# Two layers of a hybrid backbone in float32 on one Trainium2 core: the first layer rebuilt, context first, with the latents' attention between the slots of the gather

## The chip, the cores and the metric

The kernel runs on one core of one Trainium2 chip. The metric is the device time of one execution in microseconds; lower is better. Everything is computed in float32.

## The reference

There are 256 context tokens and 256 latent tokens of 1024 elements. Both go through layer 0; layer 1 gives only the latents on. In either layer a token mixer comes first and then the PEER channel mixer, which looks up experts.

```python
# layer 0 mixer: latent attention, 8 heads; context tokens read context only
a = h @ w_in                                   # 1024 -> 384 + 256 + 64
q = rmsnorm(cq) @ w_uq; kv = rmsnorm(ckv) @ w_ukv
s = q_nope @ k_nope.T + rope(q_rope) @ rope(k_rope).T
y = softmax(s * scale) @ v @ w_o; x = x + g_a * y
# layer 1 mixer: grouped-query attention, 8 heads on 2 key heads
# after either mixer: PEER, 8 heads, 16 experts of 16384 for each token and head
t = modulate(rmsnorm(x)); q = t @ w_query
v1, i1 = top_k(q[0] @ sub_k1.T, 16); v2, i2 = top_k(q[1] @ sub_k2.T, 16)
top_s, expert = top_k(v1[:, None] + v2[None, :], 16)
act = gelu(sum(t * u_tab[expert])); x = x + g_f * sum(softmax(top_s) * act * v_tab[expert])
```

The shifts, scales and gates come from silu(c) and silu(c_ctx) times a (1024, 6144) matrix for each layer ("ada"). The latents' attention in layer 0 reads the context's keys and values, but nothing of the context's PEER, so the order of the two is free there.

## The kernel before

The 512 tokens are four chunks of 128: 0 and 1 are context, 2 and 3 latents. The program is a row of phases, with a barrier of all engines behind each.

- `adaln` (L157) loads 8 MB of ada weights (8 tiles of 1 MB, one round) and makes the shift and scale of layer 0's first norm. The row vector goes to DRAM and comes back broadcast over the partitions (`modd`).
- `mla_in` (L300) normalises and transposes all four chunks and projects them with `w_in` (L337).
- `mla_attention` (L552) makes the values (L597) and then, for 8 heads, the queries and keys (L656) and for each of 32 (head, chunk) pairs scores (L457), a maximum (L532), an exponential (L504), transposes (L466) and values (L476). Between the pairs TensorE takes the other 40 ada tiles (L134), three at a time in buffers in `h` and in `arena`.
- `peer(0)` (L694) projects with `w_o` (L847), norms, transposes (L862), makes the first queries and scores (L871, L879) and the first choices of experts, all chunk by chunk, and then runs a loop over 32 units. A unit is one (head, chunk): 16 slots, each a gather by GpSimd (L833) of 128 rows of 8 KB (a row of u and one of v side by side) into one of 16 ring places.
- `gqa_in`, `gqa_attention` and `peer(1)` do layer 1 with 16 units.

Inside a unit the slots go by groups of four (`GRP`). VectorE takes the four dot products of u with the token (L1132); ScalarE the gelu (L979); VectorE multiplies by the gates (L1138); ScalarE writes four 128x128 diagonal matrices (L984), in 8 buffers; TensorE multiplies each with the slot's v rows in two matmuls of 512 columns (L924), which sum 16 slots in one pair of banks; its end frees the places. The choice of the unit after next runs on VectorE in four stages between the groups (L1019 to L1054). `add_output` (L1114, L1117) adds a unit's banks to x. The order of heads is outermost and the chunk inner, so that each unit has its own sum. The loop is a hardware loop of 4 turns of 8 units (`Fori`). In it SyncE loads a tile of the query weights (0.5 MB) and of the keys for half of the units, and TensorE turns each into scores of all four chunks (L886, L894).

```python
                        for g in range(NG):
                            pe.wait_ge(diag_ready, it * (body * NG) + i * NG + g + 1)
                                for n in range(2):
                                    last = nc.tensor.matmul(acc[i % 2][n][:], diag[:, (g % 2) * GRP + k, :], ring[:, kk, D + n * 512:D + (n + 1) * 512],
                                                            start=(kk == 0), stop=(kk == TOPK - 1))
                            last.then_inc(slots_free, 1)
```

## Time and profile before

| what | value |
| --- | --- |
| runs | 2618.32, 2620.34, 2622.73 us; median 2620.34 |
| profiled execution | 2617.42 us, its span 2615.7 us |
| PE busy | 2126.6 us, 81% of the span |
| VectorE busy | 1776.3 us, 68% |
| ScalarE, GpSimd busy | 582.4 us (22%), 848.5 us (32%) |
| DMA moved | 919.71 MB, 352 GB/s in the mean, 805.36 MB of it by the gathers |
| mean granted TensorE clock | 0.924 of 2.4 GHz |

PE is TensorE's matmuls, DVE VectorE, ACT ScalarE, POOL GpSimd and SP SyncE. A float32 matmul of 128 rows stands in the records as two, so 16 records are 8 matmuls. The profile's page cuts the span in 40 slices of 65.4 us; a digit is a tenth of it busy. A wait that the trace calls "issue" is time in which an engine waited for nothing that the profile shows.

### The profile page before, as it was taken

The numbers are of one execution on the slowest core, as the hardware profiler recorded it, in microseconds if no ns is written. First come the engines' busy times: TensorE is split into PE (matmuls) and PEld (weight loads), VectorE is DVE, ScalarE is ACT, GpSimd is POOL, SyncE is SP. The second block draws the span as 40 slices with busy tenths as digits, with TensorE's granted clock in tenths as the row PEclk, the third lists the DMA queues.
The fourth block names the chain that finished last, engine by engine and source line by source line (L and its number), as shares of the span: only waits on it lengthen the run. The fifth ranks groups of instructions, "written<-read, shape, count | busy, mean of one in ns | idle before, by whom it ended". The sixth has DMA issues, their size and how long they took to land. (4 is left out here: it accounts for less than half of the span.)

```text
span 2615.7 us, 21115 instructions
## 1 busy us (share of the span) xinstructions
PE 2126.6 (81%) x5856; PEld 999.3 (38%) x5856; DVE 1776.3 (68%) x4349; ACT 582.4 (22%) x1533; POOL 848.5 (32%) x774
## 2 busy tenths in 40 slices
PE   5899888888778887788877888777859878698786
PEld 2444454333333333333333333334534333344343
DVE  2223357877778877788786887835468777688686
ACT  1222122222212122122212212122212212121212
POOL 0000023443444434444443444200035344254341
PEclk8999999999889998899988999988979989899898
DMA  8467457999999999999999999932179999999996
GB/s 336 157 221 267 173 199 321 421 421 420 422 383 421 421 420 422 376 421 422 420 421 377 421 421 421 404 124 101 41 312 421 420 407 421 410 397 421 387 421 253
DMA packets 136073, 919.71 MB, mean 352 GB/s; under 512 B 15744, under 2 KB 20864, under 8 KB 30128
## 3 DMA queue, kind: packets, MB, share of 16 engines
q0 software_dynamic: 110592, 805.36, 74.5%
q1 hardware_dynamic: 24960, 113.03, 11.5%
q8 instruction: 24, 0.39, 0.1%
q14 instruction: 65, 0.53, 0.1%
q10 hardware_dynamic: 432, 0.40, 0.0%
HBM read 917.58 MB, written 1.15 MB: 351 GB/s over the span
## 5 line engine op out<-in xcount | busy, mean ns | idle before, releaser
L924 PE MATMUL bank<-arena,aux 128*128 128x512 f32 x3072 | 1454.6, 631 | 367.6 <-ACT aux L984 367.5
L833 POOL DMA_INDIRECT arena<-in_uv,small x768 | 848.0, 1104 | 1241.3 <-PE bank L924 941.8
L924 PEld LDWEIGHTS bank<-arena,aux 128*128 128x128 f32 x3072 | 608.8, 202 | 1178.4 <-issue 720.0
L1132 DVE CUSTOM_DVE_ANT_0 arena<-arena,h 128x1024 f32<-128x1024 f32 x768 | 904.6, 1223 | 147.0 <-DMA arena<-in_uv,small 86.3
L979 ACT ACTIVATE small<-small 128x4 f32<-128x4 f32 x192 | 39.4, 205 | 1349.0 <-DVE small L1132 1349.0
L984 ACT ACTIVATE aux<-ident,small 128x128 f32<-128x128 f32 x768 | 245.3, 390 | 59.7 <-DVE small L1138 59.4
L886 PE MATMUL bank<-hT,aux 128*128 128x512 f32 (+1 forms) x512 | 170.3, 486 | 0.0
L822 POOL IOTA small<- 128x16 int32 x2 | 0.3, 134 | 477.5 <-POOLq L53 477.5
L886 PEld LDWEIGHTS bank<-hT,aux 128*128 128x128 f32 x512 | 97.4, 190 | 74.5 <-issue 68.8
L1053 DVE RECIPROCAL small<-small 128x1 f32<-128x1 f32 x52 | 8.5, 164 | 133.6 <-ACT small L992 131.5
L1114 DVE TENSOR_TENSOR bank<-bank,aux 128x512 f32<-128x512 f32 x96 | 67.2, 700 | 47.0 <-PE bank L924 40.5
L847 PE MATMUL bank<-arena,hT 128*128 128x512 f32 x192 | 83.4, 593 | 3.3 <-PEq L53 3.3
L457 PE MATMUL bank<-arena 128*128 128x512 f32 (+1 forms) x160 | 67.5, 539 | 2.1 <-PEq L53 1.4
L1138 DVE TENSOR_TENSOR small<-small 128x4 f32<-128x4 f32 x192 | 31.4, 163 | 54.9 <-ACT small L979 54.9
L1117 DVE TENSOR_TENSOR x<-x,bank 128x512 f32<-128x512 f32 x96 | 65.9, 687 | 3.3
L1132 DVE DVE_READ_ACCUMULATOR2_ANT small<- 128x1 f32 x768 | 63.2, 82 | 0.0
L532 DVE TENSOR_REDUCE small<-bank 128x1 f32<-128x512 f32 (+1 forms) x48 | 28.8, 601 | 50.3 <-PE bank L457 50.3
L979 ACT ACT_TABLE_LOAD x48 | 61.6, 1283 | 1.8 <-PE bank L879 1.0
L992 ACT ACT_TABLE_LOAD x48 | 61.6, 1283 | 0.8
L1233 PE MATMUL bank<-arena,hT 128*128 128x512 f32 x128 | 57.8, 611 | 2.9 <-ACT hT L243 2.9
L656 PE MATMUL bank<-arena 128*128 128x512 f32 x128 | 56.3, 593 | 0.8 <-DVE arena L608 0.8
L1022 DVE MAX8 small<-aux 128x8 f32<-128x128 f32 x156 | 52.9, 339 | 5.4
(143 smaller groups left out, 1420.9 us busy)
## 6 DMA issues: line engine op xcount, KB each, us to landing
h<-in_ada SPq DMA_DIRECT2D x27, 1024.0 KB, 6.0
arena<-in_ada SPq DMA_DIRECT2D x21, 1024.0 KB, 6.9
aux<-in_w_query SPq DMA_DIRECT2D x36, 512.0 KB, 7.9
arena<-in_uv,small POOLq DMA_INDIRECT x768, 21.3
arena<-mod_rows SPq DMA_DIRECT2D x17, 512.0 KB, 6.3
arena<-in_w_o SPq DMA_DIRECT2D x2, 4096.0 KB, 12.1
arena<-in_w_qkv SPq DMA_DIRECT2D x3, 2048.0 KB, 13.0
arena<-in_w_in SPq DMA_DIRECT2D x2, 1536.0 KB, 8.3
```

The costliest lines, as they stand in the source:

```text
L457: last = nc.tensor.matmul(self.bank[S_BANK[u % 2]][:, 0:keys_of(c)], q, k, start=(i == 0), stop=(i == len(terms) - 1))
L833: nc.gpsimd.indirect_dma_start(out=ring[:, k, :], out_offset=None, in_=table, in_offset=bass.IndirectOffsetOnAxis(ap=idx[:, i % 2, k:k + 1 ...
L847: last = nc.tensor.matmul(self.bank[2 * (i % 2) + n][:], self.hT[:, hd, c * P:(c + 1) * P], self.w_o[:, hd, n * 512:(n + 1) * 512], start= ...
L886: last = nc.tensor.matmul(Q_BANK[:, lo:hi], wq[:, k, :], self.hT[:, k, lo:hi], start=(k == 0), stop=(k == KD - 1))
L924: last = nc.tensor.matmul(acc[i % 2][n][:], diag[:, (g % 2) * GRP + k, :], ring[:, kk, D + n * 512:D + (n + 1) * 512], start=(kk == 0), st ...
L979: nc.scalar.activation(w[:, u, ks], a[:, u, ks], ACT.Gelu).then_inc(gelu_done, 1)
L984: last = nc.scalar.mul(diag[:, (g % 2) * GRP + k, :], self.ident[:], w[:, u, g * GRP + k:g * GRP + k + 1])
L992: nc.scalar.activation(gate[:, u, :], top, ACT.Exp, bias=nb, accum_out=es).then_inc(exp_done, 1)
L1114: link(nc.vector.tensor_tensor(s, s, gate_f[:, kind(chunks[c]), n * 512:(n + 1) * 512], ALU.mult))
L1117: link(nc.vector.tensor_tensor(xs, xs, acc[u][n][:], ALU.add))
L1132: last = nc.vector.tensor_tensor_reduce(out=ring[:, k, 0:D], in0=ring[:, k, 0:D], in1=self.h[:, chunks[c] * D:(chunks[c] + 1) * D], scale= ...
L1233: last = nc.tensor.matmul(self.bank[3 * (i % 2) + n][:], self.hT[:, k, c * P:(c + 1) * P], self.w_qkv[:, n, k, :], start=(k == 0), stop=(k ...
```

## The change

Phases 1 to 4 (`adaln`, `mla_in`, `mla_attention`, `peer(0)`) become one phase, `trunk`, without a barrier in it and without a hardware loop. Layer 1 stays as it is, line for line.

- **Context first.** Only chunks 0 and 1 are normed, projected and attended ahead of the first unit (8 heads, each for both context chunks at once). All 48 ada tiles are taken in this part, 8 first, 10 in the projections and 3 in each of 10 steps of the attention; they use 7 places and from tile 35 on 3. `x` is loaded between ada tiles 3 and 4.
- **Queues.** The stores of the modulation rows and the broadcast loads of the context part go from SyncE to GpSimd. `w_o` is loaded twice (whole behind ada tile 34, then for the latents in four parts of 1 MB), each head's `w_uq` and `w_uk` twice (0.5 MB a head), and each query tile of layer 0 twice (16 MB where 8 MB were).
- **Units.** Of the 32 units the 16 of the context come first, and the chunk is outermost: units 0 to 7 are chunk 0, 8 to 15 chunk 1, then 2 and 3. The 8 units of a chunk sum into one pair of banks, and the chunks alternate between two pairs (banks 0, 1 and banks 2, 3), so `add_output` runs 4 times and no more 32 times.
- **Combine.** The diagonals stay 128x128. There are 4 buffers, written one by one; TensorE waits for two, does 4 matmuls and frees two ring places.
- **Ring.** GpSimd waits before each gather. Gathers use 7 places in units 0 to 2, 10 up to unit 15 and 15 from unit 16 on.
- **Latents between slots.** `Turns` gives out the latents' work at positions: position 2k is in the k-th group (behind the first pair on TensorE, behind the second dot product on VectorE), position 2k + 1 at its end. Norm transposes at 1 and 3, projections at 5 to 16, values at 18 and 20, head 0 from 22, heads 3 to 7 one in 6 positions from 50 on, `w_o` at 83 to 90, the second norm at 91 to 104. A unit is 8 positions. So the latents' part fills units 0 to 12.
- **Queries.** `job_of` gives queries of one head for two chunks: heads 2 to 7 of the context in units 0 to 4, the latents' heads in units 13 to 20, each 32 matmuls of 256 columns. The tops of a head's second chunk are kept in `vals`.

```diff
+    def run(self, position):
+        while self.due is not None and self.due <= position:
+            self.due = next(self.program, None)
...
+        for n in range(SLOTS):
+            pos = n % 7 if n < 48 else n % 10 if n < SLOTS // 2 else n % 15
+            self.turn.append(1 + self.place.count(pos))
+            self.place.append(pos)
+            self.freed_by.append(holder.get(pos))
+            holder[pos] = n
...
-            self.adaln()
-            self.layer(0)
-            self.layer(1)
+            self.trunk()
+            self.gqa_in()
+            self.gqa_attention()
+            self.peer(1, list(range(CC, NC)))
...
@@ trunk, SyncE @@
+                for n in range(15, steps):
+                    ada(n)
+                    if n == 34:
+                        sp.wait_ge(ada_used, 32)
+                        sp.dma_start(self.w_o_first, d["w_o0"]).then_inc(w_o_loaded, 16)
+                    if n >= 24 and n % 3 == 0 and (n - 24) // 3 + 4 < H:
+                        sp.wait_ge(kp_done, (n - 24) // 3 + 1)
+                        head((n - 24) // 3 + 4, False)
...
+                def part(i):
+                    sp.dma_start(self.w_o_part[i], d["w_o0"][:, :, 256 * i:256 * i + 256]).then_inc(part_loaded[i], 16)
...
+                sp.wait_ge(kp_done, H + 6)
+                part(0)
+                sp.wait_ge(evac_done, 1)
+                part(2)
+                sp.wait_ge(kp_done, 2 * H)
+                part(1)
@@ trunk, GpSimd @@
+                    pool.wait_ge(rows_done, r + 1)
+                    self.ada_store(layer, i, rows[r % 2], pool, stored)
...
+                    pool.wait_ge(stored, 16 * NQ * (r + 1))
+                    if r == 0:
+                        for j, seg in enumerate((SC_A, SH_A)):
+                            pool.dma_start(self.mix_rows[:, j], self.mod_row(0, CON, seg)).then_inc(mix_ctx_loaded, 16)
...
+                for n in range(SLOTS):
+                    unit, k = divmod(n, TOPK)
...
+                    pos, prior = self.place[n], self.freed_by[n]
+                    if prior is not None:
+                        pool.wait_ge(slots_free, prior // 2 + 1)
...
+                    nc.gpsimd.indirect_dma_start(
+                        out=ring[:, pos, :], out_offset=None, in_=table,
+                        in_offset=bass.IndirectOffsetOnAxis(ap=self.idx[:, unit % 4, k:k + 1], axis=0)).then_inc(gathered[pos], 16)
@@ trunk, TensorE @@
+                ctx_proj(0)
+                for u in range(H + 2):
+                    if u < H:
+                        ctx_scores(u)
+                    if u + 1 < H:
+                        ctx_proj(u + 1)
+                    if 1 <= u <= H:
+                        ctx_transposes(u - 1)
+                    if u >= 2:
+                        ctx_values(u - 2)
+                    for n in range(18 + 3 * u, 21 + 3 * u):
+                        ada(n)
...
+                    for hd in range(3, H):
+                        b = 50 + 6 * (hd - 3)
+                        yield b
+                        scores_of(hd)
+                        yield b + 1
+                        values_of(hd - 1)
+                        if hd + 1 < H:
+                            yield b + 2
+                            q_of(hd + 1)
+                            yield b + 3
+                            k_of(hd + 1)
+                        yield b + 4
+                        transposes_of(hd)
...
+                            pe.wait_ge(diag_ready, s + 2)
...
+                                    last = nc.tensor.matmul(bank[2 * (n // H % 2) + m][:], self.dg[:, (s + o) % 4, :], ring[:, at, D + 512 * m:D + 512 * m + 512],
+                                                            start=first and o == 0, stop=last_one and o == 1)
+                            last.then_inc(slots_free, 1)
+                            if half == 0:
+                                fill.run(2 * (n * NG + g))
...
+                        elif j is not None:
+                            if g < 2:
+                                query_job(j, g)
+                            if g == 2:
+                                score_job(j)
+                        fill.run(2 * (n * NG + g) + 1)
@@ trunk, ScalarE @@
+                    def exps(hd):
+                        act.wait_ge(mx_done, H + hd + 1)
+                        if hd:
+                            act.wait_ge(pt_done, H + 2 * hd)
...
+                        for k in range(g * GRP, (g + 1) * GRP):
+                            s = n * TOPK + k
+                            if s >= 4:
+                                act.wait_ge(slots_free, (s - 4) // 2 + 1)
+                            nc.scalar.mul(self.dg[:, s % 4, :], ident[:], self.w[:, n % 2, k:k + 1]).then_inc(diag_ready, 1)
...
+                        fill.run(2 * (n * NG + g))
@@ trunk, VectorE @@
+                    def maxima(hd):
+                        dve.wait_ge(s_done, H + hd + 1)
...
+                    for hd in range(3, H):
+                        b = 50 + 6 * (hd - 3)
+                        yield b + 1
+                        maxima(hd)
+                        yield b + 3
+                        normalise(H + hd, probs_lat, TOK)
+                        if hd + 1 < H:
...
+                                op0=ALU.mult, op1=ALU.add, accum_out=self.a[:, u, k:k + 1])
+                            if k % GRP == 1:
+                                fill.run(2 * (n * NG + g))
...
+                        ks = slice(g * GRP, (g + 1) * GRP)
+                        dve.wait_ge(gelu_done, n * NG + g + 1)
+                        nc.vector.tensor_tensor(self.w[:, u, ks], self.w[:, u, ks], self.gate[:, n % 4, ks], ALU.mult).then_inc(w_ready, 1)
+                        if g == 0 and n % H == 0 and n:
+                            dve.wait_ge(slots_free, n * H)
+                            add_output(c - 1)
```

What moved shows in the order of the instructions. First TensorE in the attention of layer 0, before; L656 projects queries and keys of a head for 512 tokens, L457 are scores, L466 transposes of probabilities, L476 values, L134 an ada tile:

```order
49 L457 MATMUL bank<-arena 128x256 x2
50 L466 MATMUL bank<-ident,aux 128x128 x4
51 L476 MATMUL bank<-aux,arena 128x128 x4
52 L134 MATMUL bank<-arena,aux 32x512 x4
53 L134 MATMUL bank<-h,aux 32x512 x4
54 L457 MATMUL bank<-arena 128x256 x2
55 L656 MATMUL bank<-arena 128x512 x8
56 L466 MATMUL bank<-ident,aux 128x128 x2
57 L476 MATMUL bank<-aux,arena 128x128 x4
58 L134 MATMUL bank<-h,aux 32x512 x4
59 L457 MATMUL bank<-arena 128x512 x2
```

TensorE for a latent head in units 6 to 9, now; L852 is the combine (4 rows a pair of slots), L746 and L747 scores, L763 values, L516 and L524 queries and keys, L754 transposes:

```order
197 L852 MATMUL bank<-arena,aux 128x512 x8
198 L746 MATMUL bank<-aux 128x512
199 L747 MATMUL bank<-arena,aux 128x512
200 L746 MATMUL bank<-aux 128x512
201 L747 MATMUL bank<-arena,aux 128x512
202 L852 MATMUL bank<-arena,aux 128x512 x4
203 L763 MATMUL bank<-h,arena 128x256 x4
204 L852 MATMUL bank<-arena,aux 128x512 x4
205 L516 MATMUL bank<-arena 128x256 x6
206 L852 MATMUL bank<-arena,aux 128x512 x4
207 L524 MATMUL bank<-arena 128x512 x2
208 L852 MATMUL bank<-arena,aux 128x512 x4
```

The attention's matmuls stood together, with ada tiles between them; now each piece of a latent head stands between two pairs of slots of the combine.

VectorE at the end of a group of dot products, before (L1138 gates, L1046 and L1048 the last stage of a choice, L1053 and L1054 gates of the next, L1058 scores out of the bank, L1132 the next dot product):

```order
367 L1137 REGISTER_ALU
368 L1138 TENSOR_TENSOR small<-small 128x4
369 L1046 SCALAR_TENSOR_TENSOR small<-small 128x16
370 L1048 TENSOR_SCALAR small<-small 128x1
371 L1142 REGISTER_ALU
372 L1053 RECIPROCAL small<-small 128x1
373 L1054 TENSOR_SCALAR small<-small 128x16
374 L1057 ISA
375 L1058 COPY aux<-bank 128x4x128
376 L1131 ISA
377 L1132 ISA arena,small<-arena,h 128x1024
```

The same place in unit 7, now (L1455 gates, L1332 and L1335 the choice, L1390 and L1391 the maxima of a latent head's scores, L1447 the next dot product):

```order
775 L1455 TENSOR_TENSOR small<-small 128x4
776 L1332 SCALAR_TENSOR_TENSOR small<-small 128x16
777 L1335 TENSOR_SCALAR small<-small 128x1
778 L1390 TENSOR_REDUCE small<-bank 128x1 x2
779 L1391 TENSOR_SCALAR small<-small 128x2
780 L1447 ISA arena,small<-arena,h 128x1024
```

Between two groups of dot products VectorE now has the maxima, which wait for TensorE's scores of that head.

## Rows read from the trace of the kernel before

**Rows 1.** The page, part 2: 40 slices of the span
```profile
GB/s 336 157 221 267 173 199 321 421 421 420 422 383 421 421 420 422 376 421 422 420 421 377 421 421 421 404 124 101 41 312 421 420 407 421 410 397 421 387 421 253
```

**Rows 2.** Windows: length, busy (instructions) of PE, PEld, DVE, ACT, POOL, PEclk, DMA, GB/s
```profile
119.00:302.00 183.00, 174.05 (x864) 88.27 (x864) 57.02 (x153) 44.12 (x113) 0.00 (x0) 1.00 0.64 236
430.00:1712.00 1282.00, 1058.97 (x2368) 457.88 (x2367) 1002.07 (x2436) 285.11 (x762) 541.45 (x490) 0.93 1.00 413
```

**Rows 3.** Timeline of SP, POOL, DVE: start, length, engine, line, operation
```profile
27.85 1.18 SPq L129 DMA_DIRECT2D mod_rows<-aux  x4
31.88 0.81 SPq L225 DMA_DIRECT2D arena<-mod_rows  x2
330.83 0.29 DVE L1019 MAX8 small<-aux 128x8 f32<-128x128 f32 x1
340.86 0.17 DVE L1046 SCALAR_TENSOR_TENSOR small<-small 128x16 int32<-128x16 f32 x1
342.22 1.08 POOL L833 DMA_INDIRECT arena<-in_uv,small  x1 [39.70 <-issue]
343.61 0.95 POOL L833 DMA_INDIRECT arena<-in_uv,small  x1 [0.31 <-issue]
```

**Rows 4.** Timeline of PE ahead of and in the attention
```profile
25.21 1.07 PE L134 MATMUL bank<-arena,aux 128*32 128x512 f32 x8 [1.42 <-DMA arena<-in_ada]
44.93 12.33 PE L337 MATMUL bank<-arena,hT 128*128 128x384 f32 x32 [0.77 <-ACT hT L243]
71.71 10.59 PE L337 MATMUL bank<-arena,hT 128*128 128x384 f32 x32 [0.72 <-ACT hT L243]
241.28 7.03 PE L656 MATMUL bank<-arena 128*128 128x512 f32 x16
250.35 1.99 PE L457 MATMUL bank<-arena 128*128 128x512 f32 x4
```

**Rows 5.** Timeline of PE from `w_o` to the first queries
```profile
302.48 20.84 PE L847 MATMUL bank<-arena,hT 128*128 128x512 f32 x48 [1.89 <-PEq L53]
323.44 1.09 PE L862 MATMUL bank<-ident,h 128*128 128x128 f32 x8
325.35 3.81 PE L871 MATMUL bank<-hT,aux 128*128 128x128 f32 x32 [0.82 <-ACT hT L957]
```

**Rows 6.** The gathers of L833 from 340 to 425 us, issue to landing
```profile
DMA to landing us min/median/max: 5.6/8.9/15.4
```

**Rows 7.** Timeline of DVE, ACT and PE in the loop of layer 0
```profile
400.13 1.22 DVE L1132 CUSTOM_DVE_ANT_0 arena<-arena,h 128x1024 f32<-128x1024 f32 x1
401.91 1.28 ACT L984 ACTIVATE aux<-ident,small 128x128 f32<-128x128 f32 x4 [0.32 <-DVE small L1138]
403.24 8.94 PE L924 MATMUL bank<-arena,aux 128*128 128x512 f32 x16 [7.70 <-ACT aux L984]
571.53 13.90 PE L924 MATMUL bank<-arena,aux 128*128 128x512 f32 x32
1706.64 8.83 PE L924 MATMUL bank<-arena,aux 128*128 128x512 f32 x16 [3.33 <-ACT aux L984]
```

**Rows 8.** Groups by line and shape, 430 to 1712 us: busy, mean ns, idle before
```profile
L924 PE MATMUL bank<-arena,aux 128*128 128x512 f32 x2000 | 946.5, 631 | 223.0 <-ACT aux L984 222.9
L1114 DVE TENSOR_TENSOR bank<-bank,aux 128x512 f32<-128x512 f32 x62 | 43.4, 700 | 20.3 <-PE bank L924 15.7
L992 ACT ACT_TABLE_LOAD x32 | 41.1, 1283 | 0.6
```

**Rows 9.** The same groups of 119 to 302 us
```profile
L532 DVE TENSOR_REDUCE small<-bank 128x1 f32<-128x512 f32 x16 | 11.1, 691 | 23.1 <-PE bank L457 23.1
```

**Rows 10.** Waits, 430 to 1700 us: who waited for whom, us in total, times, longest
```profile
DVE arena L1132 <- issue: 17.6, 3, 5.9
```

**Rows 11.** Window over one end of a turn of the loop, columns as in rows 2
```profile
720.00:760.00 40.00, 25.88 (x56) 11.54 (x57) 30.14 (x75) 6.31 (x21) 10.93 (x10) 0.79 0.92 364
```

1401 lines of the change are left out of this document (1111 added, 290 removed).

## The prediction

> **What bounds the kernel now.** The page's slices come first [rows 1]. They show 421 GB/s in most slices from 8 to 25 and again from 31 on: there the gathers set the pace. Ahead of slice 7 the rate is a half of that or so, since no gather can start. The windows by stage say the same in numbers [rows 2]: 413 GB/s in the 1282 us of the first layer's units, with PE busy 1059 us of them; 236 GB/s in its attention, where PE is busy 174 of 183 us. The timelines then give the edges [rows 3, 5, 7]: the first gather is issued at 342.2, the first combine starts at 403.2, and the last one of layer 0 ends at 1715.5. A gather moves 1.049 MB, so it takes 2.49 us at 421 GB/s, and a unit of 16 takes 39.9 us. So there are two things to win: an earlier first gather, and the DMA that lies idle ahead of it. And there is one to lose: PE, which the latents' attention must now share with the combine.
>
> The profiled execution has a span of 2615.7 us and took 2617.4; the median of the runs is 2620.3. I sum the change of the span and take it off the median.
>
> **Up to the context's attention.** `x` (2.1 MB, 5 us at 421 GB/s) now goes ahead of four ada tiles, so the eighth tile, at 25.2 [rows 4], comes at 30. The four row stores and two broadcast loads are GpSimd's: a gather is issued every 1.25 us there, on SyncE four stores took 1.18 and two loads 0.81 [rows 3], which makes 7.5 against 2.0, 6 us more (below 0, if a plain transfer issues as fast as on SyncE). So the first normed chunk comes 11 us later, at 53. Then: transposes and copies 3, the first 16 matmuls of 384 columns 12.3 and the second 10.6 [rows 4], 10 ada tiles at 1.0, eight value matmuls of 512 columns at 0.87, small transposes 2.7, first head's projection 3.4. The last of it ends near 103, where the attention of all four chunks starts now at 119 [rows 2].
>
> **The context's attention.** Costs by columns come from 7.03 us for 8 matmuls of 512 columns and 1.99 for two [rows 4]. A step has scores 1.7, projections of the next head 3.4, transposes 0.5, values 0.9 and three ada tiles 3.0: 9.5 us. Ten steps, the outer ones shorter, make 79. ScalarE and VectorE have under 3 us of work in a step, beside it. DMA is not beside it throughout: `w_o` (4.2 MB, 10 us) stands ahead of tile 35 in the queue, 5 us beyond the step that hides it; from tile 35 on three places let 3.1 MB be reloaded only as they are used, which the last three steps, short of other work, don't cover (10 us); waits for the row bank 4. It ends near 201, against 302.
>
> **To the first combine.** Three times 8 matmuls of `w_o` take 20.8, and the first norm, made beside the last 8, ends with them, since the transposes follow at once [rows 5]. Transposes, copies, queries and scores take 7 as now, from 323.4 to 330.4; the choice runs 10.2 from the first maximum to the indices [rows 3]. First gather near 240, 102 us sooner. The first dots wait for VectorE's other chunk and for the fourth gather (5.6 us to land at best [rows 6]), the first combine starts near 257, 146 us sooner. That is more than will be kept.
>
> **Units 0 to 12.** The combine of a unit is 32 matmuls; 13.9 us for 16 back to back [rows 7] make 27.6. The mean over the loop is 0.95 us each [rows 8], 30.3, but with waits in it and clock 0.93; where PE was busy throughout the clock was 1.00 [rows 2], so I take 27.6. In unit 0 come on top first queries 3.8, two query jobs 14, scores 3, latents' transposes and projections 13, and VectorE must make two whole choices between its dots: 68 us. Units 1 and 2 have 7 ring places. There a group of four can't be complete before the pair ahead of it is combined: gelu, gates and two diagonals 1.2 us (from the last dot's end at 401.35 to half of the four diagonals), the pair 3.5, GpSimd's issue 0.8, landing 5.6, last dot 1.2 [rows 6, 7]: 12.3 us a group, 50 a unit, 55 for unit 1 with its two pieces of projection of 5.3 in one group.
>
> For the landing the Trainium skill, "DMA: Bandwidth & Descriptors", section "Anatomy of one DMA — SWDGE (gpsimd) path", fits 2.0 us plus bytes over 436e3 per us, 4.4 us for this gather. The trace never shows under 5.6; by the page these eight groups would be 10 us shorter in all, and the time 2573.
>
> A latent head costs PE queries 2.6, keys 1.7, scores 3.5, transposes 1.1 and values 1.7, so 10.6; all of the latents' work, by the same prices, is 145 us: 85 for the heads, 28 for `w_o`, 21 for the projections, 7 for the values and 4 of small transposes. A head has 3 groups, whose combine is 20.7. To these 31.3 I add 4 of idle PE: VectorE stands for the scores (position b + 1), and then the maxima (two reductions, 1.5 with the scaling [rows 9]), four dots (4.7) and the 1.2 to the diagonals go by, 7.4 us, while PE has a pair and the values, 5.2. That is 2.2; for the exponential with two table loads of 1.28 [rows 8] I take 1.8 more. So 35 us for 3 groups, 47 a unit in units 6 to 9. Units 3 to 5 hold 44, 41 and 41 of PE's work (pieces of heads 0 to 3, and a query job in the first two); with 3 or 4 idle they are 47, 45 and 45. Unit 10, with five eighths of `w_o`, is 49, then 42 and 41. Sum of units 0 to 12: 68 + 55 + 50 + 457 = 630, where the gathers alone would take 519. Beside them from unit 1 on the queues carry head weights 3.1, `w_o` 4.2, rows 2.6 and query jobs 14.2 MB, 57 us in all and 35 of it in these units. Unit 13 starts near 887.
>
> **Units 13 to 31.** VectorE has 31.7 us a unit now (1002 over the 31.65 units that 1282 us hold at 40.5). It loses 2.8 of `add_output` and gains 3.7, a third of a choice, in the eight units with two tops: 33. PE has 27.6 and 7.8, 35 at most. So DMA bounds. Eight units carry a query job, 1.18 MB, 2.8 us: 42.7. Eleven take 39.9. Together 781, and 10 for the three places where VectorE waits for the end of a chunk. Here is what the straight program saves: three times VectorE stands for up to 5.9 us of "issue" [rows 10], at the ends of turns, and DMA falls to 364 GB/s over 40 us, 5.4 us lost [rows 11]; the slices have three such dips, 383, 376 and 377 [rows 1]. That is most of what makes 413 out of 421. It occurs nowhere else in the loop, and in the attention, which is straight code, PE is busy 95 in 100 [rows 2], so I take none in the unrolled units. Its bounds are 0 and, if each stretch of a turn's length pays it again, 18 us.
>
> The Trainium skill, "Runtime: NRT & Kernel Launch", section "Instruction fetch mechanics", says that straight code is fetched ahead and a taken branch out of the window is not. By it the end is at 0 of these bounds; no run here shows the straight program yet.
>
> `add_output` falls from 32 to 4, 2.8 us of VectorE each (four operations of 0.70 [rows 8]), 78 us in all; DMA bounds the units where it went, so I cost it at nothing. Twice loaded weights (8.4 + 4.2 + 4.2 MB) are 40 us of DMA; half is in the slack of units 0 to 12, the rest in the 42.7.
>
> **Sum.** 887 + 791 = 1678 for the last combine of layer 0, where 1715.5 stands: 37 us less. What follows is unchanged. 2620.3 - 37 = **2583 us**.
>
> **The rivals.**
> (A) DMA bounds already from unit 1 on: the latents hide wholly. Then 325 + 31 times 39.9 + 57 = 1619, 96 us less, **2524**. For it: PE's sum of 45 us a unit is near DMA's 42 to 44. Against: PE, VectorE and ScalarE hand work to each other in fixed order with at most ten places of ring, and the place waits alone give 50 in units 1 and 2.
> (B) The hand-offs cost the whole chain. If at the scores and again at the probabilities PE runs dry for all 7.4 us, a head costs 14.8 of idle PE and not 4: 8 times 10.8 = 86 more, **2669**, slower. For it: before, with nothing between, PE already waited 223 us for diagonals in 31 units [rows 8], 7 a unit, only harmless. Against: ScalarE's gelu is mostly ready before TensorE asks. It turns the sign when a head costs 4.6 us more than I take (37 over 8).
> (C) The start isn't won: ada tiles over three places run one after the other, 13 us a step in the last five (3 times 2.5 and 5.6 to land), and the row traffic on GpSimd is late; some 35 us more, **2618**, no change to speak of.
> (D) The change doesn't do what it says, with the first gather no sooner than 300 because a context step takes twice the 9.5 us: 2640 and more.
>
> **How the numbers follow.** My forecast (2553 to 2612) has 0.46, A 0.15, C 0.16 (half of it faster), B 0.20, D 0.03. The likeliest is 2583. The range for 8 in 10 goes from 2524, A, to 2655, which takes in C and the milder half of B and the bounds of the unknown costs (GpSimd's issue 6, landing 10, instruction fetch 18). A measurement of this kernel can tell 0.2%, 5 us, from no change: faster 0.70, same 0.07, slower 0.23.
>
> **What would show it.** First gather at 225 to 255 (else C or D). First combine at 245 to 275. GB/s in units 1 and 2 near 320, in units 3 to 11 at 360 to 390 with PE above 9 tenths and clock 1.00; at 421 there it is A, under 340 with PE under 8 tenths and long waits for diagonals it is B. Units 13 on at 421 without the three dips. Layer 1 as long as now, 900 us from the last combine. I am wrong if the first layer's end does not come between 1620 and 1750, or if units from 13 on are bound by anything but DMA.

## The result, and the profile after

The change made the kernel slower: 2640.5 us (median of 5 runs, 2634.5 to 2649.4) against 2622.7 of the kernel before beside it on the chip (5 runs, 2618.3 to 2623.8), a ratio of 1.0078 with a 95% interval of 1.0051 to 1.0105. Forecast was 2583, faster. The time lies in the range, the direction was wrong. The profiled execution took 2634.5 us, its span 2632.7, so it stands 6 under the median.

**The page.** Part 2, 40 slices of 65.8 us; the row that answers to [rows 1] is the last.

```profile
PE   3987988988889889788877778867949878698787
PEclk7999999999999999899999999988979989899898
GB/s 372 312 352 179 302 272 352 370 357 347 371 361 411 365 419 403 369 419 419 421 421 421 421 421 422 421 146 97 44 284 417 420 411 420 420 400 421 389 421 239
```

Gathers now run from slice 4 on, where they ran from slice 6. But where the kernel before had 421 from slice 8 at once, here slices 5 to 12 stand at 272 to 371: eight slices in which DMA is not the bound. Slices 14 (365) and 17 (369) are low too; the second takes in the end of unit 15, where the ring changes its size. From slice 18 to the end of layer 0 it is 419 to 422: the three dips of [rows 1], at the ends of the loop's turns, are gone.

**Edges.** The timeline of TensorE: end of the context's attention with `w_o`, the first combine, the last combine of layer 0. Columns as in [rows 5].

```profile
208.04 1.60 PE L146 MATMUL bank<-arena,aux 128*32 128x512 f32 x8 [0.57 <-DMA arena<-in_ada]
209.57 20.87 PE L657 MATMUL bank<-arena,hT 128*128 128x512 f32 x48
...
268.39 7.10 PE L852 MATMUL bank<-arena,aux 128*128 128x512 f32 x16 [2.99 <-ACT aux L1135]
...
1725.16 8.58 PE L852 MATMUL bank<-arena,aux 128*128 128x512 f32 x16 [5.11 <-ACT aux L1135]
```

L146 is an ada tile and L657 the context's `w_o`. The first combine comes at 268.4 where it came at 403.2 [rows 7]: 135 us won. The last one of layer 0 ends at 1733.7 where it ended at 1715.5: 18 us lost. So 153 us went between these two points. Layer 1 takes 899 us behind it (2632.7 - 1733.7) and took 900.

**Where they went.** Windows of the change over units 0 to 2 and over units 3 to 12, both counted by their gathers, and over a stretch of units 22 to 30; columns as in [rows 2].

```profile
268.00:453.00 185.00, 163.62 (x516) 92.61 (x516) 106.26 (x301) 48.32 (x120) 52.01 (x48) 0.95 0.79 301
433.00:914.00 481.00, 423.95 (x1179) 219.41 (x1177) 321.31 (x779) 141.25 (x333) 181.12 (x160) 0.96 0.94 369
1300.00:1650.00 350.00, 273.85 (x558) 112.54 (x559) 235.96 (x526) 77.99 (x209) 157.70 (x138) 0.92 1.01 421
```

In the last stretch DMA bounds, as forecast. Ahead of it nothing is full: in units 3 to 12 TensorE is busy 88 in 100, DMA gives 369 of 421 GB/s, VectorE is busy 67 in 100. A stretch in which every engine has time left is one of waits. The waits of 268 to 915 us (who waited for whom, us in total, times, longest):

```profile
POOL arena L474 <- PE bank L852: 384.9, 85, 16.4
PE bank L852 <- ACT aux L1135: 77.9, 36, 5.4
DVE arena L1447 <- DMA arena<-in_uv,small: 71.7, 40, 5.9
DVE small L1390 <- PE bank L747: 48.9, 8, 9.6
DVE aux L1244 <- ACT aux L1042: 26.4, 6, 8.8
DVE small L1191 <- ACT aux L897: 12.7, 1, 12.7
DVE small L1255 <- ACT h L1056: 10.4, 5, 3.7
```

GpSimd waits 385 us for the combine to free a ring place, so a late combine makes the next gathers late. TensorE waits 78 us for diagonals (L1135). VectorE, which by its dots should be ahead, stands 49 us for the latents' scores (its `maxima`, L1390, waits for TensorE's L747), 26 for ScalarE's copy of a head's queries (`rotate_lat`, L1244), 10 for the exponentials, and 12.7 in one place for the squares of chunk 3 (L1191).

**One head, in full.** TensorE's timeline of head 2, from the group in which its scores stand (position 44, in unit 5) to the scores of head 3:

```profile
583.85 1.02 PE L746 MATMUL bank<-aux 128*128 128x512 f32 x2
...
587.28 3.60 PE L852 MATMUL bank<-arena,aux 128*128 128x512 f32 x8
594.96 5.34 PE L852 MATMUL bank<-arena,aux 128*128 128x512 f32 x8 [4.08 <-ACT aux L1135]
600.14 2.75 PE L516 MATMUL bank<-arena 128*128 128x256 f32 x12
602.73 3.60 PE L852 MATMUL bank<-arena,aux 128*128 128x512 f32 x8
606.16 1.88 PE L524 MATMUL bank<-arena 128*128 128x512 f32 x4
609.63 3.70 PE L852 MATMUL bank<-arena,aux 128*128 128x512 f32 x8 [1.58 <-ACT aux L1135]
...
618.92 3.70 PE L852 MATMUL bank<-arena,aux 128*128 128x512 f32 x8 [1.28 <-ACT aux L1135]
```

and VectorE's three stops in the same head:

```profile
587.55 1.42 DVE L1390 TENSOR_REDUCE small<-bank 128x1 f32<-128x512 f32 x2 [3.43 <-PE bank L747]
598.28 0.17 DVE L1255 RECIPROCAL small<-small 128x2 f32<-128x2 f32 x1 [3.72 <-ACT h L1056]
603.41 0.43 DVE L1244 TENSOR_TENSOR aux<-bank,aux 128x256 f32<-128x256 f32 x1 [3.70 <-ACT aux L1042]
```

VectorE gets the maxima at 587.55, when TensorE has just made the scores. TensorE then has one pair, 3.6 us, and runs dry for 4.08 us. The pair behind that wait takes 5.34 us where the one before took 3.60: at 595 us the granted clock is at its lower level, 1.2 GHz, as this window says (PEclk 0.50):

```profile
594.90:597.00 2.10, 2.04 (x3) 1.01 (x4) 0.00 (x0) 2.07 (x5) 0.00 (x0) 0.50 0.94 378
```

So this head has 6.9 us of idle and 1.7 of slow clock in its three groups, and these three groups take 38.6 us, from 580.31 to 618.92.

Head 2 is one of the three heads (0 to 2) that have no piece of values behind their scores. From head 3 on, as in the order ahead of the prediction, the values of the head before stand there. Head 4, whose scores start at 659.84:

```profile
663.27 3.60 PE L852 MATMUL bank<-arena,aux 128*128 128x512 f32 x8
666.70 1.89 PE L763 MATMUL bank<-h,arena 128*128 128x256 f32 x8
670.96 3.70 PE L852 MATMUL bank<-arena,aux 128*128 128x512 f32 x8 [2.37 <-ACT aux L1135]
684.15 3.70 PE L852 MATMUL bank<-arena,aux 128*128 128x512 f32 x8 [1.58 <-ACT aux L1135]
```

The wait behind the scores is 5.15, 5.15 and 4.08 us in heads 0 to 2, and 2.35, 2.37, 2.38 and 2.71 in heads 3 to 6. From scores to scores heads 3 to 6 take 37.4, 35.6, 38.0 and 37.5 us, with 4.6 us of idle in the mean.

**Units 3 to 5 and units 6 to 9, counted by their combines:**

```profile
454.80:609.60 154.80, 135.36 (x376) 71.11 (x376) 107.08 (x289) 42.41 (x103) 55.35 (x50) 0.94 0.90 360
609.60:802.10 192.50, 167.32 (x448) 81.31 (x448) 130.90 (x314) 64.69 (x151) 71.50 (x63) 0.97 0.95 367
```

TensorE is idle 19.4 us of the first and 25.2 of the second.

### The profile page after: what moved, and what is told of

Its sections match the earlier page's. It is cut to its first block and busy times, and to the rows that moved or that the text cites. A ratio compares the mean times of both kernels' runs of the same rounds, so it can differ in the third digit from the quotient of the medians.

```text
span 2632.7 us, 21000 instructions
## 1 busy us (share of the span) xinstructions
PE 2130.6 (81%) x6128; PEld 1067.8 (41%) x6128; DVE 1664.6 (63%) x4077; ACT 609.5 (23%) x1577; POOL 903.2 (34%) x837
## 2 busy tenths in 40 slices
DMA packets 164795, 936.65 MB, mean 356 GB/s; under 512 B 17184, under 2 KB 50208, under 8 KB 60240
## 5 line engine op out<-in xcount | busy, mean ns | idle before, releaser
L852 PE MATMUL bank<-arena,aux 128*128 128x512 f32 x2048 | 986.1, 635 | 232.6 <-ACT aux L1135 232.6
L474 POOL DMA_INDIRECT arena<-in_uv,small x512 | 590.9, 1154 | 893.9 <-PE bank L852 750.3
L1447 DVE CUSTOM_DVE_ANT_0 arena<-arena,h 128x1024 f32<-128x1024 f32 x512 | 613.1, 1224 | 291.8 <-DMA arena<-in_uv,small 287.3
L852 PEld LDWEIGHTS bank<-arena,aux 128*128 128x128 f32 x2048 | 405.8, 203 | 768.7 <-issue 485.3
L1970 PE MATMUL bank<-arena,aux 128*128 128x512 f32 x1024 | 487.8, 633 | 134.9 <-ACT aux L2030 134.9
L1879 POOL DMA_INDIRECT arena<-in_uv,small x256 | 279.7, 1093 | 431.7 <-PE bank L1970 324.6
L2178 DVE CUSTOM_DVE_ANT_0 arena<-arena,h 128x1024 f32<-128x1024 f32 x256 | 301.2, 1223 | 52.3 <-DMA arena<-in_uv,small 25.6
L1135 ACT ACTIVATE aux<-ident,small 128x128 f32<-128x128 f32 x512 | 164.4, 390 | 40.2 <-DVE small L1455 29.5
L530 PE MATMUL bank<-hT,aux 128*128 128x256 f32 (+1 forms) x512 | 110.6, 372 | 1.4 <-ACT hT L889 1.4
L530 PEld LDWEIGHTS bank<-hT,aux 128*128 128x128 f32 x512 | 94.4, 196 | 24.7 <-issue 12.4
L146 PE MATMUL bank<-arena,aux 128*32 128x512 f32 x312 | 47.2, 711 | 31.1 <-DMA arena<-in_ada 21.8
L141 POOL DMA_DIRECT2D mod_rows<-aux x24 | 12.2, 514 | 144.4 <-DVE aux L1181 89.6
L2272 PE MATMUL bank<-arena,hT 128*128 128x512 f32 x128 | 57.5, 609 | 2.9 <-ACT hT L1539 2.9
L1932 PE MATMUL bank<-hT,aux 128*128 128x256 f32 x256 | 57.9, 379 | 0.0
L1932 PEld LDWEIGHTS bank<-hT,aux 128*128 128x128 f32 x256 | 48.6, 190 | 13.4 <-issue 7.7
L1455 DVE TENSOR_TENSOR small<-small 128x4 f32<-128x4 f32 x128 | 20.9, 164 | 51.4 <-ACT small L1129 51.4
```

The costliest lines, as they stand in the source:

```text
L474: nc.gpsimd.indirect_dma_start(out=ring[:, pos, :], out_offset=None, in_=table, in_offset=bass.IndirectOffsetOnAxis(ap=self.idx[:, unit % ...
L530: last = nc.tensor.matmul(Q_BANK[:, side * 256 + at:side * 256 + at + width], weights[:, k, :], hT[:, k, lo:lo + width], start=(k == 0), s ...
L852: last = nc.tensor.matmul(bank[2 * (n // H % 2) + m][:], self.dg[:, (s + o) % 4, :], ring[:, at, D + 512 * m:D + 512 * m + 512], start=fir ...
L1135: nc.scalar.mul(self.dg[:, s % 4, :], ident[:], self.w[:, n % 2, k:k + 1]).then_inc(diag_ready, 1)
L1447: last = nc.vector.tensor_tensor_reduce(out=ring[:, at, 0:D], in0=ring[:, at, 0:D], in1=h[:, c * D:(c + 1) * D], scale=1.0, scalar=0.0, op ...
L1879: nc.gpsimd.indirect_dma_start(out=ring[:, k, :], out_offset=None, in_=table, in_offset=bass.IndirectOffsetOnAxis(ap=idx[:, i % 2, k:k + 1 ...
```

## The experiments

Twelve kernels, each timed beside the kernel before on the same chip. The change itself was not timed again beside them; its five runs spread over 15 us, so a difference to it of under some 7 us says nothing. "Unit" in the table is the time between the first gathers of two units (the timeline of GpSimd, L474), which run some ten slots ahead of the combine. The first two columns of numbers are time and ratio; then the length of units 0 to 2, 3 to 10 and 11 to 12, and the end of layer 0's last combine, all from each kernel's own profiled execution. These spread: six kernels whose units 0 to 2 are the change's or nearly so have 183 to 192 us there, and the change's own profiled execution, 6 us under its median, is at the low end. Differences under 8 us in that column say nothing.

| kernel | median us | ratio to before (95%) | 0-2 | 3-10 | 11-12 | last combine |
| --- | --- | --- | --- | --- | --- | --- |
| the change | 2640.5 | 1.0078 (1.0051 to 1.0105) | 184.1 | 386.3 | 95.2 | 1733.7 |
| e1 heads 3 to 7 out | 2623.2 | 1.0006 (0.9994 to 1.0017) | 190.7 | 367.0 | 94.9 | 1721.4 |
| e2 ten places from slot 32 | 2647.5 | 1.0100 (1.0075 to 1.0126) | 183.3 | 392.5 | 94.4 | 1745.6 |
| e3 stops one later | 2621.6 | 0.9999 (0.9981 to 1.0016) | 178.0 | 373.2 | 93.8 | 1716.9 |
| e4 eight diagonals | 2650.2 | 1.0102 (1.0069 to 1.0134) | 190.1 | 388.3 | 94.6 | 1748.1 |
| e5 eight places | 2707.6 | 1.0331 (1.0314 to 1.0348) | 192.0 | 430.2 | 99.8 | 1803.3 |
| e7 stops later still | 2606.9 | 0.9943 (0.9924 to 0.9961) | 184.5 | 354.8 | 93.8 | 1705.0 |
| e8 and the tail | 2603.9 | 0.9940 (0.9922 to 0.9957) | 175.1 | 354.0 | 94.9 | 1699.9 |
| e9 an eighth of `w_o` | 2638.3 | 1.0063 (1.0046 to 1.0080) | 189.5 | 386.3 | 87.3 | 1734.5 |
| e10 places, in order | 2624.2 | 1.0007 (0.9997 to 1.0016) | 173.2 | 395.0 | 88.8 | 1723.5 |
| e11 e8 and e10 | 2581.6 | 0.9850 (0.9836 to 0.9863) | 166.6 | 360.2 | 90.1 | 1680.2 |
| e12 e8, eight places | 2684.4 | 1.0230 (1.0214 to 1.0246) | 191.4 | 410.4 | 105.6 | 1786.5 |
| e13 e8, ScalarE back | 2606.6 | 0.9930 (0.9913 to 0.9947) | 184.2 | 357.6 | 94.5 | 1708.8 |

Theory 1 was: the pieces of a latent head that VectorE and ScalarE get in the same group as TensorE's piece make VectorE stop for TensorE, so that its lead over the combine is gone. Theory 2: the ring has too few places. Theory 3: four buffers of full diagonals tie ScalarE to TensorE.

**e1, the heads' price.** Edit, alike on all engines (of the heads' weights only the first four are loaded):

```
-                    for hd in range(3, H):
-                        b = 50 + 6 * (hd - 3)
-                        yield b
-                        scores_of(hd)
...
-                    values_of(H - 1)
+                    yield 51
+                    values_of(2)
```

> Leaves out heads 3 to 7 of the latents' attention in layer 0, on all engines, with the loads of the weights of heads 4 to 7 (2.1 MB); the output is not the reference's. It prices what the heads cost where they lie, in units 6 to 10. Theory 1 (TensorE's own added work plus the pieces that ScalarE and VectorE get in the same group and stop in, 12.9 us of unit for a group with head work where the gathers alone want 10): units 6 to 9 fall from 50.9, 51.4, 48.4, 48.6 to 41 or so, the first layer ends 35 to 50 us sooner, time 2590 to 2605. Theory 2 (the ring of ten places alone makes these units slow, the heads lie beside it): units 6 to 9 stay above 46, time down by less than 12 us.

Measured: 17 us less than the change, units 3 to 10 from 386 to 367. Neither theory's number. At my 10.6 us a head this took 53 us of TensorE's work away and left units of 45.9 us (367.0 over 8), not 41. What stands there without heads is in the same kernel's slices: 419 and 417 GB/s from 655 to 786 us. There the gathers and `w_o`'s parts already bound, with ten places of ring. The heads could win back no more than lay above DMA.

**e2, places sooner.** `n < 48` became `n < 32` in `ring_places`.

> Seven places of the ring only for slots 0 to 31, ten from slot 32 on (the three places are free by then), so that unit 2 has ten. Theory 2 (places bound units 0 to 2, 12.3 us a group and more): unit 2 falls from 66.9 to 50 to 55, and 8 to 15 us of it are kept to the end. Theory 1 (in unit 2 the waits of VectorE and TensorE on pieces of the latents' attention, 12.7 us at the mean of chunk 3 in one place, bind): unit 2 falls by under 5 us, time unchanged within 3.

Measured: no gain; units 1 and 2 were 86.3 and 41.2 where the change has 61.0 and 66.9, the same sum. I read this first as a mark against theory 2. It was a bad test: 32 modulo 10 is 2, and place 2 had been given to slot 30, so slot 32 had to wait until slot 30 was combined. More places came with an order that asked for one freed two slots before. e10 repeats the edit with a right order.

**e3, stops one group later.**

```
-                        yield b + 1
+                        yield b + 2
                         maxima(hd)
-                        yield b + 3
+                        yield b + 4
                         normalise(H + hd, probs_lat, TOK)
                         if hd + 1 < H:
+                            yield b + 5
                             rotate_lat(hd + 1)
```

and on ScalarE `q_copy` and `k_copy` at b + 4, `pt_copies` at b + 6, chunk 3's squares at 14, its mean at 15, its transposes at 17 and the first values at 19.

> No work left out: the pieces of VectorE and ScalarE of heads 3 to 7 are put one group later against TensorE's (maxima b + 2, normalise b + 4, rotate b + 5; copies of queries and keys b + 4, of the transposed probabilities b + 6), and the mean and squares of chunk 3 likewise one group later. Theory 1 (the engines ahead of TensorE lose their lead in pieces that wait for a piece of the same group): units 6 to 9 and unit 2 lose 3 to 5 us each, time 15 to 30 us less. Rival (TensorE's own work and the ring bind, who waits where does not matter): within 5 us.

Measured: 2621.6, 19 us less than the change: theory 1's number, with no operation added or removed. Counted by combines, units 6 to 9, whose heads were shifted, fell from 192.5 to 181.1, and unit 1, with chunk 3's mean, from 64.9 to 58.5; units 3 to 5, whose heads were not, took 155.3 where they took 154.8. VectorE's wait for the scores fell to 36.0 us in 7 waits, the 12.7 for chunk 3's squares to 4.4.

**e4, eight buffers of diagonals.** `self.dg` got four more, `s % 4` became `s % 8` from slot 48 on, with the wait for `(s - 8) // 2`.

> Eight buffers of diagonals from unit 3 on instead of four, so that ScalarE can make those of the next pairs ahead. Theory 1 and 2 expect no change (ScalarE stood for a diagonal's buffer 5 times and 10.3 us in all over the first units): within 3 us. Rival 3 (four full diagonals tie ScalarE to TensorE, so TensorE's 80 us of waits for diagonals over units 0 to 12 come from there): 15 us or more less.

Measured: 2650.2, no gain; its interval overlaps the change's. Theory 3 is out: that there are only four buffers costs nothing here. What a full diagonal costs against a smaller one, no run tests.

**e5, eight places instead of ten.** `n % 10` became `n % 8`.

> The change with eight places of the ring in units 3 to 15 instead of ten. Theory 2 (places bind there, each group waits for a place to be freed and a gather to land): two places less cost 1.5 to 3 us a unit, 20 to 35 us in all. Theory 1 (TensorE's work and the hand-offs bind, up to unit 12, and ten places were more than was used): under 10 us, and that in units 13 to 15, where DMA binds.

Measured: 67 us more, far over what theory 2 itself had said, and theory 1's "under 10" is wrong. Windows of e5 over units 3 to 12:

```profile
442.00:972.00 530.00, 437.71 (x1179) 224.03 (x1178) 327.03 (x788) 141.69 (x338) 176.76 (x160) 0.93 0.88 335
```

Against the change's 481.00 this is the same busy time of TensorE but for 14 us of lower clock, and 35 us more idle. A unit is 53.0 us there. A unit of 16 slots on 8 places turns the ring twice, so one turn takes 26.5 us in the mean: from the issue of a gather over landing, dot, gelu, gate, diagonal and combine to the place's next gather. That turn is no constant of the kernel, since the stops are in it. The shortest unit of e5 in this stretch is 46.0, a turn of 23.0; on ten places this would be 36.8 us a unit, below DMA's 39.9, and the mean one would be 42.4, above it. The change itself has units of 40.2 and 40.7 in this stretch. So ten places are enough where nothing stops and have little left over for a stop; eight are too few even without one, as units 13 and 14 show, which have no piece of the latents' attention in them. The change and e5:

```profile
936.60:1022.80 86.20, 77.91 (x209) 40.49 (x209) 59.69 (x151) 18.84 (x51) 36.27 (x31) 0.92 1.01 419
991.60:1086.30 94.70, 78.57 (x209) 40.39 (x209) 59.99 (x150) 18.92 (x51) 37.98 (x32) 0.93 0.94 378
```

**e7 and e8, stops later still.** e7 is e3 with VectorE's maxima at b + 3, normalise at b + 5, rotate at b + 6, and heads 0 to 2 alike:

```
-                    yield 36
+                    yield 37
                     maxima(1)
-                    yield 38
+                    yield 39
                     normalise(H + 1, probs_lat, TOK)
-                    yield 41
+                    yield 43
                     rotate_lat(2)
```

e8 also sets the latents' `add_mix` at 93, their norm at 95 and 96 and the transposes at 98 and 101.

> No work left out: on top of the shifts of e3, VectorE's pieces of heads 3 to 7 one position later again (maxima b + 3, normalise b + 5, rotate b + 6), and those of heads 0 to 2 one or two later than in the change, with ScalarE's exponentials to match. If VectorE's stops in front of TensorE's pieces (still 2.1 to 9.7 us at each head in e3) are what is left of the hand-offs' price, another 8 to 15 us come off, time 2605 to 2615 and faster than the kernel before. If e3 has already taken what there was, and TensorE's own work and DMA bind now, within 5 us of e3.

> As e7, and the residual and second norm of the latents' chunks, behind the latents' w_o, one or two positions later on VectorE, ScalarE and TensorE (add at 93, norm at 95 and 96, transposes at 98 and 101). VectorE stood 5.0 and 1.6 us for w_o there in e1. Expected 2 to 5 us less than e7; no change if DMA covers it.

Measured: 2606.9 and 2603.9, both faster than the kernel before; the tail's 3 us lie within the runs' spread. The waits of e7 from 268 to 884 us, and its window over units 3 to 12:

```profile
DVE arena L1446 <- DMA arena<-in_uv,small: 117.2, 71, 6.4
DVE aux L1241 <- ACT aux L1042: 9.3, 2, 7.1
DVE small L1387 <- PE bank L747: 2.9, 1, 2.9
```

```profile
435.00:884.00 449.00, 413.72 (x1177) 218.38 (x1176) 324.65 (x783) 141.76 (x334) 189.29 (x161) 0.97 0.98 397
```

The wait for the scores went from 48.9 to 2.9 us. What VectorE waits for now is the gathers (71.7 before, 117.2 now), as in a loop that DMA bounds, and GB/s rose from 369 to 397. Counted by combines, units 3 to 5 take 134.2 us where the change and e3 took 155, and units 6 to 9 take 183.0. So it is in e8. Windows of e7 and of e8 over units 3 to 5 by their combines, on ten places:

```profile
454.70:588.80 134.10, 129.25 (x376) 69.45 (x377) 107.07 (x294) 39.68 (x98) 59.56 (x49) 0.99 1.00 408
449.10:581.30 132.20, 127.31 (x376) 68.87 (x377) 106.47 (x290) 39.02 (x98) 64.75 (x49) 1.00 1.01 412
```

In e7 head 2 shows it on TensorE: from its scores to those of head 3 there is one wait of 1.72 us, where the change had three with 6.94, and it takes 31.2 us (570.81 to 602.01) instead of 38.6.

```profile
588.85 7.03 PE L852 MATMUL bank<-arena,aux 128*128 128x512 f32 x16
595.72 1.04 PE L754 MATMUL bank<-ident,h 128*128 128x128 f32 x8
598.47 3.70 PE L852 MATMUL bank<-arena,aux 128*128 128x512 f32 x8 [1.72 <-ACT aux L1132]
602.01 1.02 PE L746 MATMUL bank<-aux 128*128 128x512 f32 x2
```

**e13, whose stops.** `q_copy`, `k_copy` and `pt_copies` back at b + 3, b + 4 and b + 5.

> e8 with ScalarE's pieces of heads 3 to 7 put back where the change has them (copies of queries at b + 3 and keys at b + 4, of the transposed probabilities at b + 5), VectorE's left where e8 has them. If it was VectorE's stops that cost the time, nothing is lost against e8 (within 4 us of 2604). If ScalarE's stops count as much, 10 us or more come back.

Measured: 2606.6, 3 us above e8 and within the runs' spread, though ScalarE now stood 30.5 us for the query projections (`ACT aux L1042 <- PE bank L516`, 7 times). So for heads 3 to 7 it is VectorE's stops that cost. For heads 0 to 2 and for chunk 3 VectorE's and ScalarE's pieces were moved together, and no run separates them there. A likely reason, not shown by a run of its own, is that ScalarE has only a gelu and four diagonals ahead of a combine, while behind a stop of VectorE four dots still have to go.

**e9, TensorE's work alone.** `for hd in range(H)` became `range(1)` in the latents' `w_o`, so most of that product is left out.

> The change with one eighth of the latents' w_o product (head 0 alone in each of the eight pieces; all loads stay; the output is not the reference's). It takes 112 of 128 matmuls of 256 columns, 24 us of TensorE, out of the four groups of units 10 and 11 in which each pair of combines is followed by a whole piece. If TensorE's own work bounds those groups (13.8 us a group, 55.1 us for the 16 gathers), they fall to 41 to 44 and the time by 10 to 15 us. If that loss is made good later anyway, by under 4 us.

Measured: 2 us less, the last case of the expectation. The four groups did fall from 55.1 to 43.1, but units 12 and 13, 40.2 and 41.6 in the change, took 44.2 and 44.5 here: of 12 us 5 were left, and the medians show 2, within the spread. Windows over units 11 and 12 by their gathers, the change and e9:

```profile
819.50:914.70 95.20, 86.04 (x261) 49.19 (x259) 63.02 (x133) 25.52 (x59) 37.26 (x32) 0.96 0.96 378
```

```profile
827.30:914.60 87.30, 65.75 (x150) 28.85 (x150) 63.19 (x133) 25.09 (x59) 35.38 (x33) 0.92 1.00 405
```

TensorE lost 20 us of work there, the two units 8, and the kernel 2. So TensorE's work did set the pace of these four groups, the only place where its pieces stand that thick. But most of what is taken away there comes back as longer units behind it: in e9 DMA gives 405 GB/s over the two units and 415 from 900 to 990 us. TensorE's sum was not the bound of the whole stretch that my table of units made of it.

**e10, places in order.**

```
-            pos = n % 7 if n < 48 else n % 10 if n < SLOTS // 2 else n % 15
+            pos = (n + 5) % 7 if n < 32 else n % 10 if n < 180 else n % 12 if n < 240 else n % 15
...
+                    elif pos < 12:
+                        pool.wait_ge(pv_done, 2 * H)
```

Twelve places can be had once the last head's values are made, since `V` lies in two of them. The shifts of n make each change of size begin with a place free for seven slots or more; the change itself, at slot 256, asked for places given out five slots before.

> The change with the ring as large as the memory allows at each time, and with its places in an order that never asks for one freed less than seven slots ago: seven places for slots 0 to 31, ten to 179, twelve to 239, then fifteen. Nothing else is changed. Theory 2, in the strength that the run with eight places gave it (67 us for two places in units 3 to 15): unit 2 becomes a unit of ten places and falls from 67 to about 55, and units 11 and 12 gain a little, 10 to 20 us in all. Theory 1 (places alone do not help as long as VectorE stops in front of TensorE's pieces, as e2 said): within 5 us.

Measured: 2624.2, 16 us less, theory 2's number. Units 1 and 2 took 114.9 together, 13 less than in the change and in e2; units 15 and 16, where the change has its five short places and 84.5, took 77.1. Counted by combines, the gains are unit 2 (57.1 to 50.6), unit 12 (40.5 to 35.5) and unit 15 (52.1 to 43.3). The last was not expected, and whether it comes from the order of the places or from having fifteen of them from slot 240 on is not separated.

**e11, both.**

> The shifts of e8 with the ring of e10, all work in place. If stops and places are separate costs, e8's 2604 less what e10 wins against the change, 2585 to 2600. If e10 wins nothing: 2600 to 2608, still faster than the kernel before.

Measured: 2581.6, 1.5% faster than the kernel before (0.9836 to 0.9863) and 59 us less than the change. The shifts alone gave 37 (e8), the places alone 16 (e10), together 59: within the spread they add, and the time is 3 us below the range expected. Its page and its last combine of layer 0:

```profile
GB/s 370 315 348 151 322 300 374 402 411 369 413 418 402 418 419 419 419 419 420 421 421 421 421 421 421 382 34 102 69 345 420 420 412 420 401 418 420 387 421 236
```

```profile
1670.93 9.24 PE L854 MATMUL bank<-arena,aux 128*128 128x512 f32 x16 [7.93 <-ACT aux L1134]
```

Its units 3 to 12 run at 403 GB/s:

```profile
419.00:869.00 450.00, 420.24 (x1206) 223.18 (x1205) 332.17 (x805) 142.68 (x341) 183.49 (x160) 0.98 1.00 403
```

**e12, eight places with the stops gone.**

> The shifts of e8 with eight places in units 3 to 15. If places are only what VectorE needs to ride over its stops for TensorE's pieces (one cost, with two ways to pay it), the shifts have taken most of the stops and two places less cost under 35 us against e8. If they cost a landing for each group whatever VectorE waits for, the 67 us come back whole: 2665 to 2675.

Measured: 80 us above e8. Two places, eight instead of ten, cost as much without the stops as with them. They are not only a cushion for the stops that a better order could replace; eight are a limit of their own, on how much is under way.

## Why the prediction was wrong, step by step

A note on a word first: the text ahead of the prediction gives a query job 32 matmuls of 256 columns; it is 32 records, 16 matmuls, and the 7 us a job that the prediction took are for these (192 records of the context's six jobs are busy 43.1 us).

| step | forecast | measured |
| --- | --- | --- |
| context's attention starts | 103 | 108.4 |
| it ends | 201 | 209.6 |
| first gather | 240 | 249.1 |
| first combine | 257 | 268.4 |
| units 0 to 2 | 173 | 186.4 |
| units 3 to 5 | 137 | 154.8 |
| units 6 to 9 | 188 | 192.5 |
| units 10 to 12 | 132 | 134.4 |
| units 13 to 31, with what stands behind | 791 | 797 |
| last combine of layer 0 | 1678 | 1734 |

Units here are counted by their combines, as the prediction's are: 64 records of L852 each, 2048 in all. The miss of 56 us is 11.4 at the start, 13.4 in units 0 to 2, 17.8 in units 3 to 5, 4.5 in units 6 to 9, 2.4 in units 10 to 12 and 6 behind them. The sum had 37 to give away, so no single step turned the sign.

**The start, 11 us late.** Its mechanism was right and C and D did not come. The row traffic on GpSimd was priced from gathers, 1.25 us for an issue. A plain one takes 0.51 (four stores 2.03, two loads 1.09):

```profile
L141 POOL DMA_DIRECT2D mod_rows<-aux x24 | 12.2, 514 | 144.4 <-DVE aux L1181 89.6
```

so that term, 7.5, was 4 us too dear. Yet VectorE's first normed chunk starts at 55.3 and stands at 57.8 instead of 53: the broadcast loads are issued at 44.88, behind 5.36 of wait for the stores, and are there 10.4 later. The attention then took 101.2 us where I had 98, with 15 us of waits for ada tiles in it (5.05 at 168.6, 3.12 at 187.9, 2.86 at 205.6 and four shorter), which is what I had given `w_o` and the last steps. The rest is a microsecond or two at each step to the first combine. No run separates this part.

**Units 0 to 2.** The prediction took 12.3 us a group of four for the way of a place, from rows of the loop before. That chain leaves out what VectorE and TensorE do between: four dots in order, pieces that go first, and a landing that is 7.7 in the median at this load and not 5.6. Units 0, 1 and 2 took 64.4, 64.9 and 57.1 where I had 68, 55 and 50. In unit 1 VectorE stands 12.7 us for chunk 3's squares, a wait for which the sum has no term. With that piece a group later unit 1 takes 56.2 to 62.2 in the six kernels that have it so (e3, e7, e8, e11, e12, e13), and with ten places unit 2 takes 50.6 (e10).

**Units 3 to 5: the step that failed most.** It is "with 3 or 4 idle they are 47, 45 and 45". The three units took 154.8 instead of 137. TensorE was idle 19.4 us in them where 11 were taken, and its lower clock cost 7.0 more (half of the time that it is busy at the lower level), for which the sum has no term; its work was near the 126 of the sum. Three things were missed. The wait behind the scores was worked out as 7.4 us of VectorE less a pair and the values. In heads 0 and 1 neither stands behind the scores, and TensorE waits 5.15 us each time; in head 2 only a pair does, and it waits 4.08. VectorE stops up to three times in a head, not once: I had counted the scores, given the exponentials 1.8, and left out the rotation, which waits for ScalarE's copy, which stands behind the diagonals and waits itself for the query projection. And I put a price on the wait alone, while the clock costs again: in units 0 to 12 TensorE is idle 84 us, and is busy 45 us at the lower level in eleven stretches behind such waits, which makes some 23 us more.

e7 shows the cause with no operation changed: with the pieces of heads 0 to 2 later (VectorE's, and ScalarE's exponentials to match), units 3 to 5 take 134.2, with 6 us of idle, less than the 137 of the forecast.

**Units 6 to 9: near the forecast, in part by luck.** Here "to these 31.3 I add 4 of idle PE" came out as 4.6 in heads 3 to 6, the wait behind the scores as 2.35 to 2.71 where I had 2.2, and the lower clock added 5.1 in the four units. The head took 37.1 where I had 35, and the units 192.5 where I had 188. My rival B had this mechanism, hand-offs that cost the chain, with a turn of the sign at 4.6 us more a head. What came in these heads was 2.1 more; the sign turned with the help of the other terms. B's full price, 2669, did not come. It got 0.20 and the case with my 4 us got 0.46. My 4 us rested on no row in which such pieces stand between slots.

**And the bound below it.** I took ten places as enough ("the place waits alone give 50 in units 1 and 2", and no term from unit 3 on), and TensorE's sum of 45 a unit as what sets the pace. e9 and e1 took 24 and 53 us of TensorE's work away for 2 and 17. e5 took two places away for 67. So TensorE's work, 42 to 48 a unit, stands beside two other limits at nearly the same height: the ring, and DMA with `w_o` and the heads' weights. Ten places are enough where nothing stops: without the stops, e8's units 3 to 5 run at 412 GB/s on them, and e1's slices at 419 and 417. With a stop in each head they are not, since GpSimd can't run further ahead. Rival A's 2524 wanted 39.9 us a unit from unit 1 on. No run comes near it: e11, the fastest, takes 441 us for units 3 to 12, and 176.4 for units 0 to 2, in which there are only seven places up to slot 31.

**Units 10 to 31.** Right within 9 us in 923. `w_o` in the four groups came as worked out: 3.6 for each piece and each pair, 55.1 for the four. Units from 13 on are DMA's, at 418 to 422 GB/s, but for unit 15: 52.1 us at 335 GB/s, 9 us more than in e10 and e11 (43.3 and 42.9), where the ring's last change of size is another. So "units from 13 on are bound by anything but DMA", a sign of being wrong, came true in one unit. The 10 us given for VectorE's waits at the ends of chunks did not come: in layer 0 `add_output` waits only behind the last unit. That the 791 came out as 797 is these two against each other, luck. The straight program loses nothing at turns: the trace has no wait of VectorE for "issue" between 430 and 1700 us, where [rows 10] had 17.6. The Trainium skill, "Runtime: NRT & Kernel Launch", section "Instruction fetch mechanics", says that straight code is fetched ahead; the trace agrees, and the bound of 18 us was not needed. What the second loading of weights (936.65 MB were moved where 919.71 were) costs by itself, no run separates.

**The landing.** In units 1 and 2 the rows say 5.3, 7.7 and 11.2 us from issue to landing (least, median, most), in units 4 to 10

```profile
DMA to landing us min/median/max: 5.5/9.2/15.9
```

By the Trainium skill, "DMA: Bandwidth & Descriptors", section "Anatomy of one DMA — SWDGE (gpsimd) path", it would be 4.4, an estimate from that section's fit of 2.0 us plus the bytes over 436e3 per us. The trace never shows under 5.3, and the median grows with the load. So a turn of the ring has to be worked out with the median at the load that it will meet, not with the shortest landing.

## What to carry to other kernels

When work is put between the steps of a pipeline, don't price it by the sum of the busiest engine. Price each piece on the engine that runs ahead by how long that engine must stand for it: VectorE's piece belongs two or three positions behind TensorE's, in a group that its lead has already covered. Moving such pieces, VectorE's and those of ScalarE and TensorE that go with them, was worth 37 us here with no operation changed, and turned a loss into a gain. Then work out the turn of the buffers, from issue to freed, and from it the time of a unit (slots of a unit over places, times the turn): if that lies near the bound, there is little slack for any stop, and a buffer can be worth more than much work. Two places were worth 67 us here, 53 us of TensorE's work 17. When a ring changes its size, look at which place the first slots ask for.

## What the runs showed of the hardware that was not expected

- TensorE falls to the lower of its two levels (1.2 GHz) behind some waits, so they are paid for a second time: behind 4.08 us of wait a pair takes 5.34 instead of 3.60, the granted clock there 0.50; behind a wait of 1.58 it takes 3.70. Two waits of one length can differ: behind 2.37 us at 671 us a pair takes 3.70, behind 2.38 at 707 us it takes 5.37. Over units 0 to 12 of the change that is some 23 us on top of 84 of idle time.
- A plain store or load issued by GpSimd takes 0.51 to 0.54 us of its time (four in 2.03, two in 1.09), against 0.94 in the median and up to 1.99 for a gather.
- A gather of 1 MB in layer 0 lands in 5.3 us at best, in 9.2 at 370 GB/s and in 23.9 where DMA is full and fifteen places are under way (median of 1300 to 1650 us). There the landing costs nothing: the units run at 421 GB/s.
